# Second table's stage: the routing-weight and gelu tiles are issued from ScalarE's queue instead of SyncE's

## The chip, the cores and the metric

The kernel runs on one core of one Trainium2 chip. The metric is device time in microseconds (us) of one execution of the whole program. Three runs of the kernel before gave a median of 2546.19 us (2545.17 to 2549.54).

## What is computed

One inference step of a one-layer encoder, in float32, for 384 tokens: 256 of a new stream (the prompt) and 8 x 16 of running streams (the sample). The layer is a pooling mixer and a differential attention, then a block of experts that are looked up by key:

```python
q = (xb @ w_pq).reshape(T, PEER_HEADS, 2, D_HALF)
s = jnp.einsum('thcd,ckd->thck', q, sub_keys)
s1, i1 = lax.top_k(s[:, :, 0], PEER_TOPK)
s2, i2 = lax.top_k(s[:, :, 1], PEER_TOPK)
...
g = jax.nn.softmax(best, axis=-1)
u = jnp.take(u_tab, eidx, axis=0)
a = jax.nn.gelu(jnp.einsum('thkd,td->thk', u, xb))
vv = jnp.take(v_tab, eidx, axis=0)
return jnp.einsum('thk,thkd->td', (g * a).astype(xb.dtype), vv)
```

There are 8 heads with 16 experts each, 16384 experts, and rows of 2048 numbers in both tables (`u_tab`, `v_tab`), 134 MB each. Only the last einsum, over the second table `v_tab`, is touched by the change.

## The kernel before, in words

The program runs its engines by hand-written lists: each engine has one function with its own instructions in order and its own waits on semaphores. SyncE (SP), ScalarE (ACT) and GpSimd (POOL) can start DMAs, each on a queue of its own. In the profile SP's is q1, ACT's q10 and POOL's q0.

For the 256 prompt tokens the experts are computed densely. The first table's stage multiplies every row of `u_tab` with every token, applies gelu and writes the result to `a_dense` in HBM. GpSimd meanwhile scatters the routing weights g into `g_dense` in HBM, zero where an expert isn't chosen. The second table's stage then computes y = (g * a) @ v_tab over all 16384 experts, in 128 **blocks** of 128 rows. For the 128 sample tokens the chosen rows of `v_tab` are gathered one expert slot at a time (128 gathers of 128 rows of 8 KB, `v_row`) and added up by VectorE.

One block m of the second table's stage, with `s = m % 4` and, for the pair j = m // 2, `par = j % 2`:

- SP loads 1 MB of `v_tab` into `vraw[s]` (`v_weights`, line 377; the profile calls the four slots `v_raw` and `raw`). A slot is free when VectorE has split block m - 4, so SP waits for `lo_done` (line 408).
- ACT rounds it to `vH[s]` (`v_hi`, line 810: `v_hi` or `ring_hi`), after TensorE has done with block m - 4 (`split_used`).
- VectorE subtracts to get the remainder `vL[s]` (line 1290: `v_lo` or `ring_lo`).
- TensorE does 24 matmuls of 512 columns (`v_step`, lines 1329 to 1331) into all eight banks.

For each pair j of blocks there is one pair of **tiles**: `g_tile` and `a_tile`, 256 KB each, two buffers each (`v_routes`, lines 381 and 382). VectorE multiplies them to `w_tile` (line 1265, behind its split of the even block 2j - 2), ACT rounds the product to `w_hi` (`w_hi`, line 815, behind `v_hi` of block 2j), and VectorE forms `w_lo` (line 1270, behind its split of block 2j - 1). Its fixed order per block is: split of block m; `w_tile` of pair m/2 + 1 if m is even, `w_lo` of that pair if m is odd; one gathered row added (line 1282, from block 4 on).

SP's list in this stage before the change is the part that matters. It first issues blocks 0 to 3 and the tiles of pairs 0 and 1 among the last `a_dense` stores, waits until all those stores have landed (line 401), and then loops:

```python
            sp.wait_ge(a_store[0], 16 * 64)
            sp.wait_ge(a_store[1], 16 * 64)
            with sp.Fori(1, P // VS) as it:
                for par in range(2):
                    sp.wait_ge(w_mult, it * 2 + (par - 1))
                    v_routes(it * 2 + par, par)
                    for q in range(2):
                        s = 2 * par + q
                        sp.wait_ge(lo_done, it * VS + (s + BASE_V - 1))
                        v_weights(it * VS + s, s)
```

So the tiles of pair j stand in q1 ahead of blocks 2j and 2j + 1, and behind blocks 2j - 2 and 2j - 1. GpSimd's gather k waits until row k - 5 has been added (`row_used`, five buffers).

Of the kernel before, what the change touches and what calls it, by code (L numbers as in the profile page):

```python
# [21 lines left out]
P = 128  # L22
# [24 lines left out]
BASE_V = BASE_U  # L47
# [31 lines left out]
TD = SEQ  # L79
# [3 lines left out]
VS = 4  # L83
# [40 lines left out]
def hybrid_layer(nc, I, O):  # L124
    F32, F32R, U32 = mybir.dt.float32, mybir.dt.float32r, mybir.dt.uint32
    ALU, ACT, AX = mybir.AluOpType, mybir.ActivationFunctionType, mybir.AxisListType
    ds = bass.ds
    ctx = ExitStack()
    with ctx:
# [6 lines left out]
        def at(name, kb, shape, dt=F32):  # L136
            return nc.alloc_sbuf_tensor_at(name, shape, dt, offset=base + int(kb * KB))
# [100 lines left out]
        gt = at("g_tile", MX, [P, 2, 2, TD])  # L238
        at_ = at("a_tile", MX + 4, [P, 2, 2, TD])
# [13 lines left out]
        Gd = nc.dram_tensor("g_dense", (P, P, TD), F32, kind="Internal").ap()  # L253
        Ad = nc.dram_tensor("a_dense", (P, P, TU), F32, kind="Internal").ap()
# [3 lines left out]
        def sem(n):  # L258
            names[n] = ctx.enter_context(nc.semaphore(n))
            return names[n]  # L260
# [5 lines left out]
        hi_done, lo_done, split_used = sem("hi_done"), sem("lo_done"), sem("split_used")  # L266
# [21 lines left out]
        a_store = [sem("a_store0"), sem("a_store1")]  # L288
        ag_in = [sem("ag_in0"), sem("ag_in1")]
# [5 lines left out]
        w_mult, wh_done, wl_done, z_done, acc_done, y_done = (sem(x) for x in "w_mult wh_done wl_done z_done acc_done y_done".split())  # L295
# [22 lines left out]
        @block.sync  # L318
        def _(sp):
            def load(n, slot, parts, free):  # L320

                sp.wait_ge(free[0], free[1])
                for dst, src in parts:
                    sp.dma_start(dst, src).then_inc(raw_ready[slot], 16)

            def weight_step(n, slot, w, kq, cols):
                load(n, slot, [(raw[:, slot, k * W:(k + 1) * W], w[(kq * KQ + k) * P:(kq * KQ + k + 1) * P, cols])
                               for k in range(KQ)], (lo_done, n + 1))

            with sp.Fori(0, NG) as g:  # L330
                for s in range(12):
                    if s == 1:
                        sp.wait_ge(x_in[NT - 1], 16)
                    blk, kq = divmod(s, 4)
                    weight_step(g * 12 + s, s % 2, I["w_in"][0], kq, ds(g * GW + DPOOL + blk * DATT, W))
            for kq in range(4):
                weight_step(BASE_POOL + kq, kq % 2, I["w_in"][0], kq, ds(0, W))
            for nb in range(4):
                for i, kq in enumerate(W_OUT_ORDER):
                    weight_step(nb * 4 + (BASE_WOUT + i), i % 2, I["w_out"][0], kq, slice(nb * W, (nb + 1) * W))  # L340

            with sp.Fori(0, 4) as nb:
                for kq in range(4):
                    weight_step(nb * 4 + (BASE_WPQ + kq), kq % 2, I["w_pq"][0], kq, ds(nb * W, W))

            def u_load(m, slot):

                sp.dma_start(rawu[slot], u_v[:, ds(m, 1), :].rearrange("p o d -> p (o d)")).then_inc(u_in[slot], 16)

            def u_next(m, slot):  # L350

                sp.wait_ge(u_turn, m * 2 + (2 - 2 * UR))
                u_load(m, slot)

            def store_gelu(m, k):

                sp.wait_ge(gelu_done, m + 3)
                sp.dma_start(Ad[ds(m, 1), :, :].rearrange("o p x -> (o p) x"), aout[:, k, :]).then_inc(a_store[k], 16)

            sp.wait_ge(split_used, BASE_WPQ + 2)  # L360
            u_load(2, 2)
            u_load(3, 3)
            for m in range(2):
                sp.wait_ge(lo_done, BASE_U + m + 1)
                u_load(m, m)
            for m in range(UR, 2 * UR):
                u_next(m, m % UR)
                if m >= 6:
                    store_gelu(m - 6, m % 2)
            with sp.Fori(2, P // UR) as it:  # L370
                for q in range(UR):
                    u_next(it * UR + q, q)
                    store_gelu(it * UR + (q - 6), q % 2)

            def v_weights(m, slot):

                sp.dma_start(vraw[slot], v_v[:, ds(m, 1), :].rearrange("p o d -> p (o d)")).then_inc(v_in[slot], 16)

            def v_routes(j, par):

                sp.dma_start(gt[:, par, :, :], Gd[ds(j * 2, 2), :, :].rearrange("q p t -> p q t")).then_inc(ag_in[par], 16)
                sp.dma_start(at_[:, par, :, :], Ad[ds(j * 2, 2), :, 0:TD].rearrange("q p t -> p q t")).then_inc(ag_in[par], 16)

            sp.wait_ge(rt_ready, ROUTED)
            v_weights(0, 0)
            v_weights(1, 1)
            for m in range(P - 6, P - 2):
                store_gelu(m, m % 2)
            sp.wait_ge(dot_done, DOTS)
            sp.wait_ge(g_scat, 16 * N_SCATTER)  # L390
            v_routes(0, 0)
            sp.wait_ge(u_turn, 2 * (P - 4) + 2)
            v_weights(2, 2)
            sp.wait_ge(u_turn, 2 * (P - 3) + 2)
            v_weights(3, 3)
            v_routes(1, 1)
            store_gelu(P - 2, 0)
            store_gelu(P - 1, 1)

            sp.wait_ge(a_store[0], 16 * 64)  # L400
            sp.wait_ge(a_store[1], 16 * 64)
            with sp.Fori(1, P // VS) as it:
                for par in range(2):
                    sp.wait_ge(w_mult, it * 2 + (par - 1))
                    v_routes(it * 2 + par, par)
                    for q in range(2):
                        s = 2 * par + q
                        sp.wait_ge(lo_done, it * VS + (s + BASE_V - 1))
                        v_weights(it * VS + s, s)
            sp.wait_ge(row_used, SLOTS)  # L410
            sp.dma_start(y_rows[NT - 1], hh[:, NT - 1, :]).then_inc(y_out, 16)
            for t in range(NT - 1):
                for half in range(2):
                    sp.wait_ge(y_done, 4 * t + 2 * half + 2)
                    cols = slice(half * 2 * W, (half + 1) * 2 * W)
                    sp.dma_start(y_rows[t][:, cols], hh[:, t, cols]).then_inc(y_out, 16)
            sp.wait_ge(y_out, 16 * (1 + 2 * (NT - 1)))
            sp.wait_ge(kv_stored, NG * 96)
            sp.wait_ge(pool_out, 16 * 9)
# [120 lines left out]
        def _(act):  # L540
# [263 lines left out]
            gelu(P - 1, 1)  # L804


            def v_hi(m, s, sets):

                act.wait_ge(v_in[s], sets * 16 + 16)
                A(vH[s], vraw[s], ACT.Copy).then_inc(hi_done, 1)  # L810

            def w_hi(j, par):

                act.wait_ge(w_mult, j + 1)
                A(wth[:, par, :, :], wt[:, par, :, :], ACT.Copy).then_inc(wh_done, 1)

            v_hi(0, 0, 0)
            w_hi(0, 0)
            v_hi(1, 1, 0)
            v_hi(2, 2, 0)  # L820
            w_hi(1, 1)
            v_hi(3, 3, 0)
            with act.Fori(1, P // VS) as it:
                for s in range(VS):
                    act.wait_ge(split_used, it * VS + (s + BASE_V - 1))
                    v_hi(it * VS + s, s, it)
                    if s % 2 == 0:
                        act.wait_ge(split_used, it * VS + (s + BASE_V))
                        w_hi(it * 2 + s // 2, s // 2)


        @block.vector
# [836 lines left out]
```

## Time and profile before

| what | value |
|---|---|
| median of 3 runs | 2546.19 us |
| the profiled execution | 2546.42 us |
| its span in the trace | 2544.8 us |
| second table's stage (first v step to last) | about 1792 to 2536 us |
| busy share of the span | PE 96%, DVE 72%, ACT 37%, POOL 42% |
| granted TensorE clock over the span | 0.993 |
| DMA, whole span | 722.77 MB, mean 284 GB/s |

The profiled execution is 1.6 us longer than its span, and 0.2 us longer than the median. Busy PE is not PE at its peak, since matmuls overlap in the records. Where a line of the profile belongs to a helper function (1329 to 1331, or 1585), it covers several stages, so the stage is read by windows of time.

### The profile page before, as it was taken

To read this page: it belongs to the slowest core of one execution; us is meant where nothing else is said; L and a number is where in the kernel's file an instruction comes from. 1 tells how busy PE (TensorE), PEld (TensorE's weight loads), DVE (VectorE), ACT (ScalarE), POOL (GpSimd) and SP (SyncE) were. 2 spreads that over 40 slices of the span, in tenths; PEclk is the share of its full clock that TensorE was granted. 3 is DMA by queue.
4 is the path that set the end of the run, shared out by engine and by line. 5 is a ranking of instruction groups with operands and counts; after the bars stand their busy time and mean duration, and the time that the engine had idled before them with its cause. 6 is when DMAs were issued, how large, how long until landed. Compare 5 with 4: busy or idle time off the path is not lost.

```text
span 2544.8 us, 41887 instructions
## 1 busy us (share of the span) xinstructions
PE 2444.6 (96%) x15891; PEld 2192.4 (86%) x15891; DVE 1833.0 (72%) x2370; ACT 943.6 (37%) x1158; POOL 1061.8 (42%) x618
## 2 busy tenths in 40 slices
PE   7989999999999999899999999999899999999998
PEld 5878777778999999899999999999787777777777
DVE  3555544554477876788877777776688898888988
ACT  5354543533333333233333333333333334333332
POOL 1020100120006777722577777871344444445441
PEclk9999999999999999999999999999999999999999
DMA  5453544486335666898999999996999999999996
GB/s 192 126 190 117 172 136 142 141 336 238 126 114 144 150 166 179 283 357 333 333 347 344 335 343 338 342 341 249 352 413 411 413 412 412 412 410 412 411 411 280
DMA packets 221525, 722.77 MB, mean 284 GB/s; under 512 B 55672, under 2 KB 105624, under 8 KB 154871
## 3 DMA queue, kind: packets, MB, share of 16 engines
q1 hardware_dynamic: 132304, 397.46, 42.8%
q0 software_dynamic: 87408, 318.89, 35.2%
q10 hardware_dynamic: 1719, 5.26, 0.6%
q8 instruction: 47, 0.77, 0.1%
q14 instruction: 47, 0.39, 0.0%
HBM read 679.70 MB, written 41.83 MB: 284 GB/s over the span
## 4 chain that ended last, share of the span: by engine, by line
PE 60%; DMA 19%; DVE 13%; issue 4%; ACT 1%; SPq 1%; POOL 1%; DVEq 1%; ACTq 0%
PE banks L1329 16%; PE banks L1331 16%; PE banks L1330 16%; DMA a_tile<-a_dense 9%; PE banks L1585 8%; DMA raw<-in_v_tab 5%; DVE h L1282 5%; DVE v_lo L1290 2%; DMA v_raw<-in_v_tab 1%; DMA raw<-in_w_out 1%; DVE ring_lo L1290 1%; DVE ring_lo L860 1%; DVEq L838 1%; DMA a_dense<-gelu_out 1%; POOL g_dense L491 1%
## 5 line engine op out<-in xcount | busy, mean ns | idle before, releaser
L1329 PE MATMUL banks<-xT_hi,ring_hi 128*128 128x256 f32 (+1 forms) x2304 | 686.1, 298 | 11.7 <-DVE gelu_out L1227 10.1
L1331 PE MATMUL banks<-xT_hi,ring_lo 128*128 128x256 f32 (+1 forms) x2304 | 664.0, 288 | 0.0
L1330 PE MATMUL banks<-xT_lo,ring_hi 128*128 128x256 f32 (+1 forms) x2304 | 663.5, 288 | 0.0
L491 POOL DMA_INDIRECT g_dense<-route,route_place x256 | 462.2, 1806 | 306.3 <-DVE route_place L1194 184.6
L528 POOL DMA_INDIRECT v_row<-in_v_tab,route_place x128 | 339.0, 2648 | 428.0 <-DVE h L1282 374.6
L781 ACT ACTIVATE ring_hi<-banks 128x1024 fp32r<-128x1024 f32 x256 | 262.5, 1026 | 625.3 <-PE banks L1585 585.8
L1236 DVE TENSOR_TENSOR ring_lo<-banks,ring_hi 128x1024 fp32r<-128x1024 f32 x256 | 313.1, 1223 | 217.1 <-ACT ring_hi L781 178.4
L1329 PEld LDWEIGHTS banks<-xT_hi,ring_hi 128*128 128x128 f32 x2304 | 439.1, 191 | 13.1 <-DVE ring_lo L1236 12.6
L1330 PEld LDWEIGHTS banks<-xT_lo,ring_hi 128*128 128x128 f32 x2304 | 439.5, 191 | 0.0
L1331 PEld LDWEIGHTS banks<-xT_hi,ring_lo 128*128 128x128 f32 x2304 | 438.8, 190 | 0.0
L860 DVE TENSOR_TENSOR ring_lo<-raw,ring_hi 128x2048 fp32r<-128x2048 f32 x72 | 165.0, 2291 | 219.9 <-ACT ring_hi L556 219.5
L1282 DVE SCALAR_TENSOR_TENSOR h<-v_row,w_values,h 128x2048 f32<-128x2048 f32 x128 | 300.2, 2345 | 0.7
L1243 DVE CUSTOM_DVE_ANT_0 u_row<-u_row,x_rows 128x2048 f32<-128x2048 f32 x128 | 290.3, 2284 | 12.1 <-DMA u_row<-in_u_tab,route_place 10.5
L485 POOL DMA_INDIRECT u_row<-in_u_tab,route_place x128 | 191.5, 1496 | 181.9 <-DVE a_dots L1243 153.2
L1585 PE MATMUL banks<-cst,raw 128*128 128x128 f32 x2032 | 264.0, 273 | 0.0
L1329 PE MATMUL banks<-ring_hi,w_hi 128*128 128x512 f32 x512 | 204.0, 398 | 25.7 <-DVE ring_lo L1290 25.7
L1585 PEld LDWEIGHTS banks<-cst,raw 128*128 128x128 f32 x2032 | 228.5, 140 | 0.0
L1329 PE MATMUL banks<-v_hi,w_hi 128*128 128x512 f32 x512 | 202.3, 395 | 13.6 <-DVE v_lo L1290 13.5
L810 ACT ACTIVATE v_hi<-raw 128x2048 fp32r<-128x2048 f32 x64 | 122.8, 1919 | 229.9 <-DMA raw<-in_v_tab 222.0
L556 ACT ACTIVATE ring_hi<-raw 128x2048 fp32r<-128x2048 f32 x72 | 137.8, 1914 | 180.5 <-PE banks L1331 136.9
L810 ACT ACTIVATE ring_hi<-v_raw 128x2048 fp32r<-128x2048 f32 x64 | 122.8, 1919 | 216.5 <-DMA v_raw<-in_v_tab 214.9
L1330 PE MATMUL banks<-ring_lo,w_hi 128*128 128x512 f32 x512 | 201.6, 394 | 0.0
(248 smaller groups left out, 4012.8 us busy)
## 6 DMA issues: line engine op xcount, KB each, us to landing
raw<-in_u_tab SPq DMA_DIRECT2D x128, 1024.0 KB
v_raw<-in_v_tab SPq DMA_DIRECT2D x64, 1024.0 KB, 15.1
raw<-in_v_tab SPq DMA_DIRECT2D x64, 1024.0 KB
raw<-in_w_in SPq DMA_DIRECT2D x160, 256.0 KB, 3.4
raw<-in_w_out SPq DMA_DIRECT2D x64, 256.0 KB, 4.8
g_dense<-zeros POOLq DMA_DIRECT2D x16, 1024.0 KB, 28.6
raw<-in_w_pq SPq DMA_DIRECT2D x64, 256.0 KB, 3.6
a_dense<-gelu_out SPq DMA_DIRECT2D x128, 128.0 KB
```

Of the source, the lines that this page charges most:

```text
L485: pool.indirect_dma_start(out=urow[i % NUB][:, :], out_offset=None, in_=I["u_tab"][0], in_offset=bass.IndirectOffsetOnAxis(ap=routeU[:, NT ...
L491: pool.indirect_dma_start(out=places, out_offset=bass.IndirectOffsetOnAxis(ap=routeU[:, t, 2, j:j + 1], axis=0), in_=route[:, t, 0, j:j + ...
L528: pool.indirect_dma_start(out=vrow[k % NVB][:, :], out_offset=None, in_=rows, in_offset=bass.IndirectOffsetOnAxis(ap=routeU[:, NT - 1, 1, ...
L781: A(ringH[:, k, g * 2 * W:(g + 1) * 2 * W], psum[:, 2 + 2 * g:4 + 2 * g, :], ACT.Copy).then_inc(u_hi_done, 1)
L810: A(vH[s], vraw[s], ACT.Copy).then_inc(hi_done, 1)
L1236: V.tensor_tensor(ringL[:, k, cols], psum[:, 2 + 2 * g:4 + 2 * g, :].rearrange("p b x -> p (b x)"), ringH[:, k, cols].bitcast(F32), ALU.su ...
L1243: V.tensor_tensor_reduce(row[:, :], row[:, :], xrow[:, :], 1.0, 0.0, ALU.mult, ALU.add, adot[:, i:i + 1]).then_inc(dot_done, 1)
L1282: V.scalar_tensor_tensor(out=acc, in0=vrow[k % NVB][:, :], scalar=wval[:, k:k + 1], in1=acc, op0=ALU.mult, op1=ALU.add).then_inc(row_used, 1)
L1329: MM(out, h1, h2, start=first, stop=False)
L1330: MM(out, h1, l2, start=False, stop=False)
L1331: return MM(out, l1, h2, start=False, stop=last)
L1585: last = TR(bank[2 + b // 4][:, b % 4 * P:(b % 4 + 1) * P], rawu[slot][:, b * P:(b + 1) * P], ident)
```

## The change

The tiles of pairs 2 to 63 are issued by ACT, on ACT's queue. The waits for the `a_dense` stores move with them: ACT has them ahead of pair 2, and SP has them no more. SP's wait on `w_mult` (that the tile's buffer has been multiplied) is dropped, since ACT has waited for the same product in `w_hi`. Pairs 0 and 1 stay with SP.

```diff
@@ SyncE @@
-            sp.wait_ge(a_store[0], 16 * 64)
-            sp.wait_ge(a_store[1], 16 * 64)
             with sp.Fori(1, P // VS) as it:
                 for par in range(2):
-                    sp.wait_ge(w_mult, it * 2 + (par - 1))
-                    v_routes(it * 2 + par, par)
                     for q in range(2):
                         s = 2 * par + q
                         sp.wait_ge(lo_done, it * VS + (s + BASE_V - 1))
@@ ScalarE @@
+            def v_routes(j, par):
+
+                act.dma_start(gt[:, par, :, :], Gd[ds(j * 2, 2), :, :].rearrange("q p t -> p q t")).then_inc(ag_in[par], 16)
+                act.dma_start(at_[:, par, :, :], Ad[ds(j * 2, 2), :, 0:TD].rearrange("q p t -> p q t")).then_inc(ag_in[par], 16)
+
@@ -820,13 +821,24 @@
             w_hi(1, 1)
             v_hi(3, 3, 0)
-            with act.Fori(1, P // VS) as it:
+            for par in range(2):
+                act.wait_ge(a_store[par], 16 * 64)
+            for par in range(2):
+                v_routes(2 + par, par)
+            with act.Fori(1, P // VS - 1) as it:
                 for s in range(VS):
                     act.wait_ge(split_used, it * VS + (s + BASE_V - 1))
                     v_hi(it * VS + s, s, it)
                     if s % 2 == 0:
                         act.wait_ge(split_used, it * VS + (s + BASE_V))
                         w_hi(it * 2 + s // 2, s // 2)
+                        v_routes(it * 2 + (s // 2 + 2), s // 2)
```

The last round of the loop is written out behind it, without `v_routes`.

SyncE's list at the end of the first table's stage and the start of the loop over the second table, before (L358 is the store of gelus, L377 a block, L381 and L382 the tiles):

```order
L377 DMA raw<-in_v_tab 128x2048 [waits u_turn] x2
L381 DMA g_tile<-g_dense 128x2x256
L382 DMA a_tile<-a_dense 128x2x256
L358 DMA a_dense<-gelu_out 128x256 [waits gelu_done] x2
L402 UNCONDITIONAL_BRANCH [waits a_store1,a_store0]
L402 ISA
L381 ISA [waits w_mult]
L381 DMA g_tile<-g_dense 128x2x256
L382 DMA a_tile<-a_dense 128x2x256
L408 ISA
L377 ISA [waits lo_done]
L377 DMA v_raw_122<-in_v_tab 128x2048
```

And with the change:

```order
L377 DMA raw<-in_v_tab 128x2048 [waits u_turn] x2
L381 DMA g_tile<-g_dense 128x2x256
L382 DMA a_tile<-a_dense 128x2x256
L358 DMA a_dense<-gelu_out 128x256 [waits gelu_done] x2
L400 UNCONDITIONAL_BRANCH
L400 ISA
L377 ISA [waits lo_done]
L377 DMA v_raw_122<-in_v_tab 128x2048
```

Block 4 (the last row) now waits for `lo_done` alone, and neither the two waits nor a tile stand ahead of it.

ScalarE's list from block 3 into its loop, with the change (L811 is `v_hi`, L816 `w_hi`, L805 and L806 the tiles):

```order
L811 ACTIVATE v_hi_125<-raw 128x2048 [waits v_in3]
L805 DMA g_tile<-g_dense 128x2x256 [waits a_store1,a_store0]
L806 DMA a_tile<-a_dense 128x2x256
L805 DMA g_tile<-g_dense 128x2x256
L806 DMA a_tile<-a_dense 128x2x256
L828 UNCONDITIONAL_BRANCH
L828 ISA
L810 ISA [waits split_used]
L811 ACTIVATE ring_hi<-v_raw_122 128x2048 [waits v_in0]
```

The tiles of pairs 2 and 3 now go out together, ahead of the rounding of block 4. Later in the same list, one half of a round:

```order
L816 ACTIVATE w_hi<-w_tile 128x512 [waits w_mult]
L805 ISA
L805 DMA g_tile<-g_dense 128x2x256
L806 DMA a_tile<-a_dense 128x2x256
L811 ACTIVATE ring_hi<-v_raw_123 128x2048 [waits v_in1,split_used]
```

Two DMA issues now stand between the rounding of the product and the rounding of the odd block.

## Rows read from the trace of the kernel before

**Rows 1.** The page's chain of waits that ended last, by line.

```profile
PE banks L1329 16%; PE banks L1331 16%; PE banks L1330 16%; DMA a_tile<-a_dense 9%; PE banks L1585 8%; DMA raw<-in_v_tab 5%; DVE h L1282 5%; DVE v_lo L1290 2%; DMA v_raw<-in_v_tab 1%; DMA raw<-in_w_out 1%; DVE ring_lo L1290 1%; DVE ring_lo L860 1%; DVEq L838 1%; DMA a_dense<-gelu_out 1%; POOL g_dense L491 1%
```

**Rows 2.** Windows: us, busy us of each engine, granted clock, DMA share, GB/s.

```profile
1840.00:2500.00 660.00, 630.75 (x2716) 509.72 (x2715) 587.98 (x345) 246.48 (x170) 318.50 (x118) 0.99 1.02 412
2500.00:2505.00 5.00, 5.00 (x23) 4.13 (x22) 4.39 (x2) 1.92 (x1) 2.55 (x1) 1.00 1.02 423
```

**Rows 3.** Waits, 1700 to 2545 us: engine, for whom: us, times, longest.

```profile
ACT v_hi L810 <- DMA raw<-in_v_tab: 222.0, 58, 8.9
ACT ring_hi L810 <- DMA v_raw<-in_v_tab: 214.9, 61, 8.7
DVE w_tile L1265 <- DMA a_tile<-a_dense: 55.2, 29, 7.3
DVE w_lo L1270 <- ACT w_hi L815: 33.3, 32, 4.4
```

**Rows 4.** Groups by line, 1820 to 2520 us: busy, mean ns, idle before.

```profile
L1329 PE MATMUL banks<-ring_hi,w_hi 128*128 128x512 f32 x483 | 191.5, 396 | 17.5 <-DVE ring_lo L1290 17.5
L1329 PE MATMUL banks<-v_hi,w_hi 128*128 128x512 f32 x480 | 189.8, 395 | 12.2 <-DVE v_lo L1290 12.1
```

**Rows 5.** DMA queues, 1900 to 2500 us: packets, MB, share of 16 engines.

```profile
q1 hardware_dynamic: 42999, 134.74, 57.1%
q0 software_dynamic: 15390, 112.06, 45.2%
```

**Rows 6.** Window 1800 to 1830 us, and the first five of it.

```profile
1800.00:1830.00 30.00, 28.03 (x124) 22.90 (x123) 24.21 (x17) 13.07 (x9) 5.49 (x2) 1.00 0.89 312
1800.00:1805.00 5.00, 3.03 (x14) 2.19 (x13) 5.00 (x4) 2.43 (x2) 0.00 (x0) 1.00 0.37 141
```

**Rows 7.** Timeline of SP's queue at the stage's start: start us, us, what.

```profile
1782.20 5.14 SPq L358 DMA_DIRECT2D a_dense<-gelu_out  x2
1803.04 0.41 SPq L381 DMA_DIRECT2D g_tile<-g_dense  x1
...
1804.24 0.96 SPq L377 DMA_DIRECT2D v_raw<-in_v_tab  x2
...
1816.89 5.80 SPq L377 DMA_DIRECT2D v_raw<-in_v_tab  x2
```

**Rows 8.** Timeline of VectorE at the stage's start; in brackets idle before, releaser.

```profile
1789.92 2.28 DVE L1290 TENSOR_TENSOR ring_lo<-v_raw,ring_hi 128x2048 fp32r<-128x2048 f32 x1
...
1806.51 0.69 DVE L1265 TENSOR_TENSOR w_tile<-a_tile,g_tile 128x512 f32<-128x512 f32 x1 [1.28 <-DMA a_tile<-a_dense]
1807.12 2.28 DVE L1290 TENSOR_TENSOR v_lo<-raw,v_hi 128x2048 fp32r<-128x2048 f32 x1
1813.83 0.69 DVE L1270 TENSOR_TENSOR w_lo<-w_tile,w_hi 128x512 fp32r<-128x512 f32 x1 [4.43 <-ACT w_hi L815]
1814.44 2.28 DVE L1290 TENSOR_TENSOR ring_lo<-v_raw,ring_hi 128x2048 fp32r<-128x2048 f32 x1
```

**Rows 9.** Timeline of ScalarE, block 4 and the product of pair 2.

```profile
1811.36 1.92 ACT L810 ACTIVATE ring_hi<-v_raw 128x2048 fp32r<-128x2048 f32 x1 [8.67 <-DMA v_raw<-in_v_tab]
1813.18 0.61 ACT L815 ACTIVATE w_hi<-w_tile 128x512 fp32r<-128x512 f32 x1
```

**Rows 10.** Timeline of TensorE, first matmul of block 1.

```profile
1802.48 0.50 PE L1329 MATMUL banks<-ring_hi,w_hi 128*128 128x512 f32 x1 [1.97 <-DVE ring_lo L1290]
```

**Rows 11.** Timeline of SP's queue and of ScalarE in steady running.

```profile
2006.99 0.42 SPq L382 DMA_DIRECT2D a_tile<-a_dense  x1
...
2006.11 0.62 ACT L815 ACTIVATE w_hi<-w_tile 128x512 fp32r<-128x512 f32 x1
2008.38 1.92 ACT L810 ACTIVATE v_hi<-raw 128x2048 fp32r<-128x2048 f32 x1 [1.65 <-DMA raw<-in_v_tab]
```

**Rows 12.** DMA in 1300 to 1400 us, first table's stage: queue and issues.

```profile
q1 hardware_dynamic: 3836, 16.09, 42.5%
...
raw<-in_u_tab SPq DMA_DIRECT2D x13, 1024.0 KB
a_dense<-gelu_out SPq DMA_DIRECT2D x14, 128.0 KB
```

More of the change, by code:

```diff
@@ L829, in _ @@
                         w_hi(it * 2 + s // 2, s // 2)
+                        v_routes(it * 2 + (s // 2 + 2), s // 2)
+            for s in range(VS):
+                act.wait_ge(split_used, P - VS + s + BASE_V - 1)
+                v_hi(P - VS + s, s, P // VS - 1)
+                if s % 2 == 0:
+                    act.wait_ge(split_used, P - VS + s + BASE_V)
+                    w_hi(P // 2 - 2 + s // 2, s // 2)
         @block.vector
```

## The prediction

> **What bounds the kernel now.** I read the chain of waits first. It names the change's own transfer: the loads of `a_tile` hold 9% of the span [rows 1], 229 us, which looks like a prize. Before believing it I ask what those loads wait for, so the windows of the second table's stage come next. From 1840 to 2500 us the 16 DMA engines are busy 1.02 of the time and move 412 GB/s, while PE shows 0.96 (630.75 of 660) and DVE 0.89 [rows 2]. A full DMA share that doesn't move for 660 us is a bound. The bytes agree: a block moves 1.049 MB of the table, 1.049 MB of gathered rows and half of 0.524 MB of tiles, 2.36 MB, which at 412 GB/s is 5.73 us, and 128 of these make 733 us of the some 744 that the stage takes. The waits say the same from the other side: ACT stands 222.0 + 214.9 us for blocks, against DVE's 55.2 us for tiles and 33.3 us for `w_hi` [rows 3]. PE's idle time in this stretch is only 17.5 + 12.2 = 29.7 us [rows 4].
>
> So the tile is late because it stands in q1 behind two blocks, two megabytes, in a stage whose DMA engines are full. If it passes them, somebody else's bytes wait.
>
> **Steady running: the rate.** The change removes no byte and no packet. SP issues the 62 pairs of tiles no more, two issues of some 0.42 us each [rows 11]; SP is on no path there. The time of the issue hardly moves either. SP begins `a_tile` at 2006.99, right behind `g_tile`; ACT would begin the two behind `w_hi`, which ends at 2006.73 [rows 11]. What moves is the queue. On q10 the tile shares the engines with q1 and q0 instead of standing behind q1's blocks, and lands sooner. DVE's 55.2 us of waits for tiles then go, and what is late next is the block: ACT waits longer for it, `w_hi` stands behind that block's rounding in ACT's list, and DVE waits at `w_lo` in place of `w_tile`. I cost steady running at **0 us**. The cover is the full DMA share; were it gone, the gain would end where PE is never idle, 29.7 us.
>
> ACT gains two issues for each of 62 pairs, about 0.9 us with the gap between them, in front of the rounding of the odd block. That rounding waited 1.65 us for its data in the sample that I read [rows 11], so this lies in idle time: **0 us**. Without that cover it would be 62 x 0.9 = 56 us, which is why it is worth watching.
>
> **The start of the stage.** Here the change takes a wait away. From 1800 to 1830 us the DMA engines move 312 GB/s, and only 141 in the first five [rows 6]. Against 412 that is 30 x (1 - 312/412) = **7.3 us of DMA time lost**. The cause is in SP's list: the last store is issued by 1787, then SP stands for the stores to land until 1803.04, and block 4 goes out at 1804.24 [rows 7]. Its slot was free when DVE had split block 0, at 1789.92 + 2.28 = 1792.2 [rows 8]. With the change it goes out there, 12 us sooner. The engines are still full then, so it queues and fills the hole as it opens.
>
> - Block 4 in the hole: 1.05 MB at 412 GB/s, **2.5 us** of DMA time.
> - The next loads: before, block 4 was rounded only at 1811.36 after 8.67 us of waiting, and `w_hi` behind it at 1813.18 [rows 9]. That held DVE 4.43 us at `w_lo` and put the split of block 4 at 1814.44 to 1816.7 [rows 8]. Block 8 is released by it, at 1816.89 [rows 7], and so is the first added row and through it gather 5. With the change block 4 lies ready. `w_hi` then waits for PE to end block 1: 1802.48 [rows 10] plus 5.4 us (24 matmuls at 28.03/124 = 0.226 us each [rows 6]), so 1807.9, and it ends at 1808.5. DVE ends its split of block 3 at 1807.12 + 2.28 = 1809.4, does `w_lo` (0.69) and the split of block 4 (2.28), and is through at 1812.3 [rows 8]. Block 8 is 4.6 us sooner. But the tiles of pair 2, alone in q1 before (1803.04 to 1806.5), now share with blocks 4 and 5, which can cost them up to a block's 2.5 us, and DVE's product at 1806.51 waits for them. So the lead is 2.1 to 4.6 us, and I take the middle, **3.4 us**.
> - The tiles pass blocks: each block lands later by what a pair of tiles takes, 0.524 MB / 412 = 1.3 us. That is one shift, not one for each pair, since the total is the same; it costs once, at the end: **-1.3 us**.
>
> PE's own start doesn't move: block 1 waits for DVE's split of it, which stands behind the product of pair 1, and those tiles stay in q1. From 1802.48 PE runs without a gap to 1830 (28.03 of the 30 us, [rows 6]). It needs 5.4 us for a block against the DMA's 5.73, so it has room to take the lead over.
>
> Sum: 2.5 + 3.4 - 1.3 = 4.6 us. At the ends: if only the small lead counts, 2.1 - 1.3 = 0.8 us; if the whole hole is filled at no cost, 7.3 us. The profiled execution took 2546.42 us, so I forecast 2546.4 - 4.6 = **2541.8 us**; the median of the runs is 0.2 us under the profiled one, which I leave out.
>
> **The rivals.**
>
> *Nothing comes of it.* The tiles change queues, the engines are the same, and what block 4 gains is eaten at once: the tiles of pairs 2 and 3, now issued together, pass blocks 4 and 5 and delay them by 2 x 1.3 us, and the shift at the end takes another 1.3. For it: both pairs come at the worst time, with DVE waiting for one of them. Against it: the hole of 7.3 us is real, and its loads are ready. From my 4.6 us another 2.6 and up to the whole 3.4 of the lead go, so 2545 to 2547, say 2546. Chance 0.10. The Trainium skill (DMA: Bandwidth & Descriptors, section Issuing engines are not separate DMA queues) states this as a rule: DMAs started by ScalarE, SyncE and GpSimd run on the same 16 DMA engines and interleave, and spreading them saves only the time of issuing. By that rule alone the sum would be 0; the full share of the steady stretch agrees with it, while the hole at the start is a matter of when SP gets to issue, which the rule allows for.
>
> *The DMA share is not a true ceiling.* DVE's late tile would then be what holds back the next loads, and 412 GB/s what the requests ask for. For it: 423 GB/s from 2500 to 2505 [rows 2], and tiles are what DVE waits for at the end of many chains. Against it: the share is full in every window. At 423 the 660 us would take 660 x 412/423 = 643, 17 us less, so 2546.4 - 4.6 - 17 = 2525; the far end is PE's 29.7 us, 2512. Chance 0.10.
>
> *A third queue makes small packets dearer: slower.* Tiles travel in pieces of 1 KB, 512 to a pair. On q0, 112.06 MB are 13,680 pieces of 8 KB, and 0.452 x 16 x 600 us make 317 ns for each. On q1 four fifths of the bytes are blocks, 13,160 such pieces; its 0.571 x 9600 us less those leave 1,310 us for some 26,300 pieces of 1 KB, 50 ns each [rows 5]. Among the scatters of the first table's stage, the same sum for 13 blocks and 14 stores leaves (680 - 527) us for 1,792 pieces, 85 ns [rows 12]. So company can change the price. Each ns more costs 512/16 = 32 ns a pair, 2 us over 62 pairs. The gain is gone at 2.3 ns more, and the change is slower by 0.2% at 5 ns. At a quarter of the way to 85 (9 ns) it costs 18 us: 2541.8 + 18 = 2560; at the far end 70 us. Against it: those were writes beside scatters of single numbers, and these are the same reads beside the same gathers as now. Chance 0.14, nearly all of it slower.
>
> **How the numbers follow.** A measurement of this kernel can tell about 0.2% from no change, 5.1 us. My own case has 0.66. Its gain runs from 0.8 to 7.3 us, around 4.6, and passes 5.1 in a little under half: 0.30 faster, 0.36 the same. The first rival adds 0.10 to the same, the second 0.10 to faster, the third 0.13 to slower and 0.01 to the same. That makes 0.40 faster, 0.47 the same, 0.13 slower. The forecast stays with its own sum, which lies just inside the same. For 8 in 10 the range takes my case (2539.1 to 2545.6), the first rival (to 2547), and a little of the other two on each side, 2535 to 2549.
>
> **What the changed profile would show.** Block 4 issued near 1792 instead of 1804.24; the window 1800 to 1830 near 400 GB/s instead of 312; `w_lo` of pair 2 and the split of block 4 some 2 to 4.6 us sooner; q10 with 33 MB more; DVE's waits for `a_tile` near nothing, those of `w_lo` longer by about as much, and ACT's for blocks unchanged at some 437 us; 412 GB/s as before in steady running; the last block's load and the end some 4 to 5 us sooner. I am wrong if the steady rate leaves 410 to 414 GB/s: upward the second rival, downward the third. I am wrong about ACT if PE comes to wait on the odd blocks more than on the even ones.

## The result and the profile after

The change makes the kernel slower: 2607.77 us (median of 4 runs, 2604.78 to 2608.68) against 2545.68 us, a ratio of 1.0243 with a 95% interval of 1.023 to 1.0255. That is 62 us, and far outside the range of 2535 to 2549. The profiled execution took 2608.68 us, its span 2607.1 us.

The two windows of [rows 2] and [rows 6] and the DMA queues of [rows 5], now. First the windows (us, busy us of each engine, granted clock, DMA share, GB/s):

```profile
1800.00:1805.00 5.00, 5.00 (x23) 4.12 (x24) 2.58 (x2) 0.88 (x2) 0.00 (x0) 1.00 1.01 402
1800.00:1830.00 30.00, 27.41 (x114) 22.26 (x115) 21.85 (x16) 10.78 (x8) 5.50 (x3) 0.94 0.90 314
1840.00:2500.00 660.00, 595.78 (x2488) 484.26 (x2487) 534.65 (x315) 229.82 (x156) 291.11 (x108) 0.95 0.96 377
```

The steady stretch, which I had costed at nothing, moves 377 GB/s instead of 412, and the DMA engines are busy 0.96 of the time instead of 1.02. The stage's 302 MB take 801 us at 377 and 733 at 412: 68 us more, somewhat over the 62 measured. From 1800 to 1830 us the rate is that of before (314 against 312), so the time was lost in steady running, by DMA engines that stand idle.

Queues, 1900 to 2500 us (packets, MB, share of 16 engines):

```profile
q0 software_dynamic: 14256, 103.82, 42.0%
q1 hardware_dynamic: 13537, 98.58, 41.7%
q10 hardware_dynamic: 25475, 24.56, 12.1%
```

q10 carried 24.56 MB in 12.1% of 16 x 600 us. That is 48 ns for each 1 KB piece, where [rows 5] gave 50 ns in q1. The DMA records of the trace, taken one by one from 1900 to 2500 us, have a mean of 48 ns in both. A small piece is not dearer on a third queue. Now the waits of [rows 3] (the lines have moved by 12 in VectorE's list):

```profile
ACT w_hi L816 <- PE banks L1343: 156.2, 37, 8.2
DVE w_tile L1277 <- DMA a_tile<-a_dense: 152.7, 24, 10.4
ACT w_hi L816 <- DVE w_tile L1277: 126.3, 24, 10.0
ACT ring_hi L811 <- DMA v_raw<-in_v_tab: 101.7, 33, 6.4
ACT v_hi L811 <- DMA raw<-in_v_tab: 97.2, 33, 6.3
```

VectorE waits 152.7 us for the tiles that were to come early, 55.2 before. ACT waits 199 us for blocks, 437 before. The blocks are early now and the tiles late.

One such wait in order of time. The chain of waits, then the timelines of ACT and VectorE (start us, us, what, in brackets idle before and releaser):

```profile
1994.96 25.28 DMA a_tile<-a_dense
...
1994.96 0.94 ACTq L806 DMA_DIRECT2D a_tile<-a_dense  x1
...
2009.96 2.29 DVE L1302 TENSOR_TENSOR ring_lo<-v_raw,ring_hi 128x2048 fp32r<-128x2048 f32 x1
2020.26 0.69 DVE L1277 TENSOR_TENSOR w_tile<-a_tile,g_tile 128x512 f32<-128x512 f32 x1 [8.01 <-DMA a_tile<-a_dense]
```

The tile takes 25 us to land. In the kernel before, such loads stand in the chain with 15 to 19 us, two of them here:

```profile
1996.06 16.20 DMA a_tile<-a_dense
...
2018.96 17.19 DMA a_tile<-a_dense
```

With the change VectorE stands for 8 of the 25 us, and since it releases the blocks and the gathers, both other queues run empty behind it. Two windows show the end of that:

```profile
2010.00:2020.00 10.00, 10.00 (x46) 8.28 (x45) 2.25 (x2) 1.92 (x1) 2.75 (x1) 1.00 1.03 418
2020.00:2030.00 10.00, 6.03 (x18) 4.48 (x17) 9.74 (x6) 4.34 (x3) 4.19 (x2) 0.74 0.66 251
```

After the stall the DMA share is 0.66, TensorE works 6 of 10 us, and its granted clock in that window is 0.74. The clock is a second part of the price, and it lies on the way to the next tile. After the stall before this one:

```profile
1986.97 0.63 PE L1341 MATMUL banks<-v_hi,w_hi 128*128 128x512 f32 x1 [3.12 <-DVE v_lo L1302]
...
1987.00:1990.00 3.00, 3.00 (x8) 2.32 (x9) 3.00 (x3) 1.87 (x1) 0.73 (x1) 0.53 0.92 313
1991.00:1994.00 3.00, 3.00 (x15) 2.48 (x14) 3.00 (x3) 0.00 (x0) 1.79 (x1) 1.00 1.00 399
```

TensorE had stood 3.12 us for VectorE's split. Its granted clock is 0.53 at first (the lower level, 1.2 of 2.4 GHz, for nearly all of it) and 1.00 from 1991 on. The first matmuls start 0.43 us apart, later ones 0.23. The block's 24 matmuls take 7.2 us (1986.97 to 1994.13) instead of the 5.4 that 24 x 0.23 make. ACT rounds the product behind them at 1994.34, and only then issues the tile of 1994.96. The chain of waits from 1840 to 2500 us has 16 such loads of `a_tile`, of 24 to 31 us. At 1.8 us each the lower clock would account for up to 29 of the 62 us. That is an estimate, and no run separates it from the wait that sets it off.

Why 25 us for half a megabyte? The queues in 2012 to 2021 us, when all three had work, and in 2022 to 2032 us, when the other two had little:

```profile
q0 software_dynamic: 235, 1.79, 47.8%
q1 hardware_dynamic: 231, 1.75, 46.9%
q10 hardware_dynamic: 217, 0.21, 6.7%
...
q1 hardware_dynamic: 148, 1.07, 26.0%
q0 software_dynamic: 118, 0.93, 22.3%
q10 hardware_dynamic: 646, 0.62, 19.6%
```

In the first window the three queues moved about the same number of pieces, 235, 231 and 217 (with a few records of 4 bytes in each), but the two others' were of 8 KB and q10's of 1 KB. That gave the first theory.

### The profile page after: what moved, and what is told of

It reads as the page before. It is cut to its first block, busy times and chain, and to the rows that moved or that the text cites. A ratio compares the mean times of both kernels' runs of the same rounds, so it can differ in the third digit from the quotient of the medians.

```text
span 2607.1 us, 41846 instructions
## 1 busy us (share of the span) xinstructions
PE 2465.8 (95%) x15891; PEld 2213.7 (85%) x15891; DVE 1829.0 (70%) x2370; ACT 948.8 (36%) x1158; POOL 1062.2 (41%) x618
## 3 DMA queue, kind: packets, MB, share of 16 engines
q0 software_dynamic: 87408, 318.89, 34.4%
## 4 chain that ended last, share of the span: by engine, by line
PE 69%; DMA 19%; DVE 8%; issue 2%; POOL 1%; DVEq 1%; ACT 0%; ACTq 0%; SPq 0%
PE banks L1341 19%; PE banks L1343 19%; PE banks L1342 19%; DMA a_tile<-a_dense 18%; PE banks L1597 8%; DVE h L1294 2%; DVE v_lo L1302 1%; DVE ring_lo L1302 1%; DVEq L850 1%; DMA a_dense<-gelu_out 1%; POOL g_dense L487 1%; DMA raw<-in_w_in 0%; DVE prm L952 0%; DVE prm L979 0%; PE banks L1548 0%
## 5 line engine op out<-in xcount | busy, mean ns | idle before, releaser
L1341 PE MATMUL banks<-xT_hi,ring_hi 128*128 128x256 f32 (+1 forms) x2304 | 686.0, 298 | 13.0 <-DVE gelu_out L1239 11.5
L1341 PEld LDWEIGHTS banks<-xT_hi,ring_hi 128*128 128x128 f32 x2304 | 439.0, 191 | 14.4 <-DVE ring_lo L1248 14.0
L1341 PE MATMUL banks<-v_hi,w_hi 128*128 128x512 f32 x512 | 208.4, 407 | 45.1 <-DVE v_lo L1302 45.1
L1342 PE MATMUL banks<-v_lo,w_hi 128*128 128x512 f32 x512 | 206.7, 404 | 0.0
L1343 PE MATMUL banks<-v_hi,w_lo 128*128 128x512 f32 x512 | 205.8, 402 | 0.0
L1343 PE MATMUL banks<-ring_hi,w_lo 128*128 128x512 f32 x512 | 205.3, 401 | 0.0
```

Source lines behind the costliest of these rows:

```text
L1341: MM(out, h1, h2, start=first, stop=False)
L1342: MM(out, h1, l2, start=False, stop=False)
L1343: return MM(out, l1, h2, start=False, stop=last)
```

## The theories

**A.** Each DMA engine takes one piece from each queue in turn. A pair of tiles is 512 pieces, 32 for each engine, so beside two full queues it needs 32 x (317 + 317 + 50) ns = 21.9 us and a latency. The stage wants a pair every 11.5 us. In SyncE's queue the tile's pieces stood one behind the other, and a pair of tiles competed with one other queue, not two.

Equal counts alone would also fit turns of several pieces each. The start times of the records settle it. Of the pieces that end between 2012 and 2021 us on q0, 86% have a q1 piece start within 5 ns of their end. Behind q1's it is a q10 piece (84%), and behind q10's a q0 piece (93%). A piece of the same queue follows in 9 to 12% of cases, which is chance. So the order is q0, q1, q10, q0, one piece each.

The tile lands with the slowest of the 16 DMA engines. From 1998 to 2002 us q10 had 485 records beside q0's 88 and q1's 66, and some 460 of the 512 pieces of the pair issued at 1994.5 had started by then. Yet the pair hadn't landed. In 2002 to 2009 us:

```profile
q0 software_dynamic: 203, 1.52, 52.0%
q1 hardware_dynamic: 185, 1.38, 47.3%
q10 hardware_dynamic: 30, 0.03, 1.2%
```

At one piece in 0.684 us these 30 are the work of about three DMA engines. (The trace doesn't name the engine of a record, so this is inferred.) The pair's first piece starts at 1998.0, and 32 turns from there end at 2019.9. VectorE starts at 2020.26. So the 21.9 us are the time of a DMA engine whose other two queues never run short. From 1840 to 2500 us the median `a_tile` landed after 18.8 us, and 21 of 52 took more than 20.

**B.** The moment of the issue costs. It now stands behind ACT's wait for TensorE (156.2 us in all). The start times in the traces speak against it. From the end of a product to the issue of the tiles that reuse its buffer it was 5.5 us in the mean before, and it is 1.5 us with the change. From there to the product that needs these tiles it was 17.3 us, and it is 23.4. So the tiles are issued earlier, and come later.

**C.** Small pieces are dearer on a third queue. That was the slower rival of the prediction; the 48 ns above speak against it.

## Experiments

All ratios are against runs of the kernel before on the same chip. Their median was 2547.49 us for the first four kernels of the table, 2545.22 us for act_512 and real_act_start, and 2547.35 us for the others. The ratio is not the quotient of the two medians, and can differ from it by 0.1%; small gains below are worked out from the ratio. All but act_512 and act_early lie within 2% of the kernel before with the whole interval.

| kernel | runs | median us | ratio, 95% interval |
|---|---|---|---|
| sp_after_whi | 8 | 2546.61 | 0.9993 (0.9981 to 1.0004) |
| act_wide | 5 | 2532.55 | 0.9933 (0.9917 to 0.9948) |
| act_half_blocks | 5 | 2557.04 | 1.0035 (1.002 to 1.0051) |
| act_early | 2 | 2587.77 | 1.0157 (1.0099 to 1.0216) |
| act_512 | 2 | 2678.29 | 1.0522 (1.0503 to 1.0542) |
| block4_first | 12 | 2542.25 | 0.9986 (0.9975 to 0.9997) |
| real_act | 6 | 2533.34 | 0.9945 (0.993 to 0.9961) |
| real_sp | 8 | 2535.52 | 0.996 (0.9947 to 0.9974) |
| real_sp_block4 | 6 | 2535.56 | 0.9958 (0.9942 to 0.9974) |
| real_act_start | 6 | 2529.67 | 0.9933 (0.992 to 0.9946) |

### The moment alone: sp_after_whi

```diff
-                    sp.wait_ge(w_mult, it * 2 + (par - 1))
+                    sp.wait_ge(wh_done, it * 2 + (par - 1))
```

> The kernel before, with one semaphore changed: SyncE issues the tiles of pair j + 2 only once ScalarE has rounded the product of pair j (as late as ScalarE does it with the change), but still in SyncE's own queue, in line with the blocks. Theory A (the queue is what costs: on a queue of its own a tile moves one 1 KB piece each time that the two other queues move 8 KB each, so it lands some 24 us after its issue instead of 16): the tiles stay in line, so this stays within 5 us of the kernel before, 2541 to 2551 us. Theory B (the moment is what costs: the issue now stands behind ScalarE's waits for TensorE, 156 us in all): this loses most of what the change loses, 2590 to 2610 us.

Measured: no difference. Its steady stretch is the old one:

```profile
1840.00:2500.00 660.00, 631.08 (x2709) 509.82 (x2708) 587.75 (x343) 245.77 (x169) 317.19 (x118) 0.99 1.02 412
```

In SyncE's queue the issue can wait for ACT's rounding and nothing is lost. As a test of B it is weak, though, since the new wait seldom held anything up. SyncE's waits, 1840 to 2500 us:

```profile
SPq L381 <- ACT w_hi L815: 11.0, 14, 1.6
```

The mean from a product to the issue went from 5.5 to 5.7 us only. What tells against B by itself is that the changed kernel has 1.5 us there.

### Half as many pieces: act_wide

```diff
-                act.dma_start(gt[:, par, :, :], Gd[ds(j * 2, 2), :, :].rearrange("q p t -> p q t")).then_inc(ag_in[par], 16)
+                act.dma_start(gt[:, par, :, :].rearrange("p q t -> p (q t)"), Gd[ds(j * 2, 2), :, :].rearrange("q (h r) t -> (q h) (r t)", r=2)).then_inc(ag_in[par], 16)
```

and the same for `a_tile`. The numbers land in other places, so this kernel shows the time only.

> The changed kernel, with the 62 pairs of tiles on ScalarE's queue read as 2 KB for each partition instead of twice 1 KB: the same bytes in half as many pieces (the numbers land in other places, so the result isn't the reference's). Theory A: half as many turns, 16 for each DMA engine instead of 32, each of 317 + 317 + about 90 ns, so 12 us and the fixed latency; the tile is no longer late, VectorE's waits for a_tile fall from 152.7 us to under 40, and the time comes back to 2540 to 2555 us. Theory B: pieces change nothing, 2600 to 2610 us. A third theory, C (a 1 KB piece costs a DMA engine more when it comes from a third queue): the DMA share stays, half of the extra goes, 2570 to 2580 us.

Measured: 75 us came back, 13 more than the change had lost. Waits for tiles, then q10 from 1900 to 2500 us:

```profile
DVE w_tile L1277 <- DMA a_tile<-a_dense: 34.4, 22, 10.2
...
q10 hardware_dynamic: 15110, 27.51, 12.1%
```

Same bytes, same queue, same issue, half the turns. A gives the direction and the 34.4 us; it does not give a time below the kernel before. That part is taken up by real_sp.

### The other queue's pieces halved: act_half_blocks

```diff
-                sp.dma_start(vraw[slot], v_v[:, ds(m, 1), :].rearrange("p o d -> p (o d)")).then_inc(v_in[slot], 16)
+                src = v_v[:, ds(m, 1), :].rearrange("p o d -> p (o d)")
+                for c in range(2):
+                    sp.dma_start(vraw[slot][:, c * 2 * W:(c + 1) * 2 * W], src[:, c * 2 * W:(c + 1) * 2 * W]).then_inc(v_in[slot], 16)
```

ACT's wait for a block counts both halves.

> The changed kernel, with each block of the second table loaded by two DMAs of half its columns: 4 KB pieces on SyncE's queue instead of 8 KB, the tiles untouched. Theory A: a turn of the three queues now takes about 317 + 160 + 50 = 527 ns instead of 684, so the tile lands after 32 x 0.527 = 17 us instead of 22 to 25; its waits fall by more than half and the time to 2550 to 2585 us (the blocks get fewer bytes a turn, so not all of it comes back). Theories B and C: no gain, 2600 us or more.

Measured: 51 us came back with the tiles untouched. This is the test I trust most, since nothing about the tiles, their queue or their issue differs from the changed kernel. The steady window and q1 from 1900 to 2500 us:

```profile
1840.00:2500.00 660.00, 626.48 (x2693) 503.94 (x2692) 580.20 (x339) 242.47 (x167) 314.88 (x117) 0.99 1.03 407
...
q1 hardware_dynamic: 29243, 106.48, 45.0%
```

The DMA share is full again, and VectorE waits for `a_tile` 3 times and 14.4 us in all. What is left, 407 against 412 GB/s, is the price of the 4 KB pieces: 4,320 us for 26,000 of them, 166 ns each, against half of 317. 302 MB at 407 take 9 us longer, and the kernel is 9.5 us slower than its kernel before.

### The issue ahead of the wait for TensorE: act_early

```diff
+                        act.wait_ge(w_mult, it * 2 + (s // 2 + 1))
+                        v_routes(it * 2 + (s // 2 + 2), s // 2)
                         act.wait_ge(split_used, it * VS + (s + BASE_V))
                         w_hi(it * 2 + s // 2, s // 2)
-                        v_routes(it * 2 + (s // 2 + 2), s // 2)
```

> The changed kernel, with ScalarE issuing the tiles of pair j + 2 as soon as pair j has been multiplied, ahead of its wait for TensorE and of the rounding. Theory A: the queue still moves one pair in 22 to 25 us whenever the other two are full, so a head start of a few us helps a part only: 2575 to 2605 us. Theory B: the late issues are gone, 2541 to 2560 us.

Measured: 20 of the 62 us came back by the median. There are two runs, 2582.11 and 2593.44 us, and the interval allows 7 to 37 us. In the faster one, VectorE still waits 124.6 us for tiles, and the DMA share is 0.98:

```profile
DVE w_tile L1278 <- DMA a_tile<-a_dense: 124.6, 21, 10.8
...
1840.00:2500.00 660.00, 608.85 (x2578) 495.79 (x2577) 556.00 (x327) 235.18 (x161) 302.42 (x113) 0.96 0.98 389
```

So the moment counts once the queue is slow, for about a third, known only roughly. The chain shows how: in the changed kernel product, issue and landing follow each other on it, and an earlier issue shortens that round.

### Twice as many pieces: act_512

Each of the tile DMAs is cut in two by columns, on both engines:

```diff
+                for c in range(2):
+                    cs = slice(c * P, (c + 1) * P)
+                    act.dma_start(gt[:, par, :, cs], Gd[ds(j * 2, 2), :, cs].rearrange("q p t -> p q t")).then_inc(ag_in[par], 16)
```

> The changed kernel with every tile DMA cut in two by columns, so that ScalarE's queue carries 512 B pieces, twice as many, of the same bytes. Theory A: a pair needs 64 turns instead of 32, each of 317 + 317 us/1000 and some 30 to 40 ns, 42 us while both other queues are full, against the 11.5 us in which the stage wants a pair; the DMA engines stand idle far more often, DMA share under 0.9, and the loss against the kernel before grows from 60 us to well over 150: 2700 to 2950 us. If instead the price of a small piece were only its own time on the engine, 512 more pieces of 30 ns are under 1 us a pair, 2610 to 2670 us.

Measured: 2678 us, 133 us over the kernel before instead of 62. The loss about doubled, but I had expected well over 150, so A's range, from 2700 us on, missed by 22 us at its near end. The other range, to 2670, missed by 8, so the time alone doesn't decide. VectorE's waits for `a_tile` rose from 152.7 to 221.8 us, and from 1840 to 2500 us the DMA share is 0.90, at 344 GB/s. My sum of turns leaves out that VectorE's stall empties the other queues and the tile then runs freely. That this is the whole reason for the miss is not shown. The turns themselves show well. Queues in 2010 to 2020 us, and two issues on ACT's queue:

```profile
q0 software_dynamic: 281, 2.04, 49.2%
q1 hardware_dynamic: 276, 2.00, 48.2%
q10 hardware_dynamic: 261, 0.13, 4.6%
...
2009.36 10.22 ACTq L809 DMA_DIRECT2D g_tile<-g_dense  x1
2019.67 2.08 ACTq L810 DMA_DIRECT2D a_tile<-a_dense  x1
```

The counts are equal again, 281, 276 and 261, with q10's pieces now of 512 B: 0.13 MB against 2.0. Half the size, half the bandwidth. The order of the starts is the same as well, q0, q1, q10, in about eight of ten.

### The start alone: block4_first

On the kernel before; the first round of the loop is written out behind this, without its block 4:

```diff
+            sp.wait_ge(lo_done, VS + BASE_V - 1)
+            v_weights(VS, 0)
             sp.wait_ge(a_store[0], 16 * 64)
             sp.wait_ge(a_store[1], 16 * 64)
```

> The kernel before, with one thing that the change did by the way and nothing else: SyncE issues block 4 as soon as block 0 has been split, ahead of its wait for the a_dense stores. The tiles stay in SyncE's queue. The prediction's own term: block 4 fills 2.5 us of the hole in the DMA traffic and the blocks behind it lead by up to 4.6 us, so 2.5 to 6 us faster than the kernel before, ratio 0.9976 to 0.999. The rival: what block 4 gains is eaten by the later blocks, ratio 0.999 to 1.001. The hole itself should show 380 GB/s or more from 1800 to 1830 us instead of 312 either way if block 4 was what it lacked.

```profile
1800.00:1830.00 30.00, 29.82 (x131) 24.68 (x132) 25.80 (x19) 13.30 (x10) 8.24 (x3) 1.00 0.99 356
...
1808.29 2.29 DVE L1300 TENSOR_TENSOR ring_lo<-v_raw,ring_hi 128x2048 fp32r<-128x2048 f32 x1
```

Measured: 0.14% faster (0.03 to 0.25%), 3.5 us, and 356 GB/s in the hole where I had written 380 or more. The split of block 4 starts at 1808.29 in this execution, 6 us before that of [rows 8], but the whole start of the stage lay some 2 us earlier here, so the lead is 4 us.

### A layout with 2 KB pieces: real_act, real_sp, real_sp_block4, real_act_start

`g_dense` and `a_dense` are laid out by partition, block, token, so that a pair's tile is one run of 2 KB for each partition. The scatter's place becomes i1 * 128 + i2, and no instruction is added:

```diff
-                V.scalar_tensor_tensor(out=place, in0=i2, scalar=float(P), in1=i1, op0=ALU.mult, op1=ALU.add)
+                V.scalar_tensor_tensor(out=place, in0=i1, scalar=float(P), in1=i2, op0=ALU.mult, op1=ALU.add)
...
-                sp.dma_start(Ad[ds(m, 1), :, :].rearrange("o p x -> (o p) x"), aout[:, k, :]).then_inc(a_store[k], 16)
+                sp.dma_start(Ad[:, ds(m, 1), :].rearrange("p o x -> p (o x)"), aout[:, k, :]).then_inc(a_store[k], 16)
...
-                act.dma_start(gt[:, par, :, :], Gd[ds(j * 2, 2), :, :].rearrange("q p t -> p q t")).then_inc(ag_in[par], 16)
+                act.dma_start(gt[:, par, :, :].rearrange("p q t -> p (q t)"), Gd[:, ds(j * 2, 2), :].rearrange("p q t -> p (q t)")).then_inc(ag_in[par], 16)
```

real_act is the changed kernel so, real_sp the kernel before so, real_sp_block4 is real_sp with block4_first's start. real_act_start is real_act with that start, and pairs 2 and 3 stay with SyncE.

> The changed kernel with g_dense and a_dense laid out by partition, then block, then token, so that a tile reads 2 KB in one piece for each partition, and all numbers are the reference's. Theory A (a queue gets turns by pieces): as with the permuted 2 KB reads, VectorE's waits for a_tile under 40 us and 2528 to 2540 us, unless the first table's stage suffers from scatters and stores that now lie further apart; that is seen in the window 1100 to 1700 us, which has 341 GB/s and a full TensorE before.

> The same layout on the kernel before: the tiles in 2 KB pieces, in SyncE's queue. From the shares of the queues a 1 KB piece costs a DMA engine about 50 ns and a 2 KB piece should cost 80 to 90, so a pair saves (512 x 50 - 256 x 85)/16 = 0.24 us less than nothing to 0.35 us, over 62 pairs 10 to 20 us: 2526 to 2537 us. If that is what the faster run with 2 KB pieces on ScalarE's queue had, the two kernels with this layout agree within 4 us, and ScalarE's queue brings nothing of its own. If its early landing is worth something by itself, this one is 5 us or more slower than the other.

> The 2 KB layout in SyncE's queue together with block 4 ahead of the store waits. If the two gains add, it is 2.5 to 6 us below real_sp and the fastest of all; if block 4 brings nothing it equals real_sp.

> The 2 KB layout with the tiles on ScalarE's queue from pair 4 on; block 4 goes out early as in block4_first, and pairs 2 and 3 stay in SyncE's queue, where pair 2 isn't held up by the blocks and gathers of two other queues (VectorE waited 11.72 us for it with the tiles of pair 2 on ScalarE's queue). If the two parts add, 5 to 8 us less than real_act, 2524 to 2530 us and the fastest of all; if the start doesn't matter, as real_act, about 2533 us. From 1800 to 1830 us it should move about 360 GB/s as block4_first does.

The steady window of real_sp and its q1, then that of real_act:

```profile
1840.00:2500.00 660.00, 634.86 (x2752) 514.80 (x2751) 595.12 (x348) 248.35 (x171) 322.39 (x120) 1.00 1.02 417
...
q1 hardware_dynamic: 29947, 136.29, 55.9%
```

```profile
1840.00:2500.00 660.00, 642.66 (x2781) 527.19 (x2781) 603.11 (x352) 254.17 (x174) 317.99 (x120) 0.98 1.02 417
```

Both have 417 GB/s at a full DMA share. By the sum of [rows 5], real_sp's pieces of 2 KB cost 86 ns where two of 1 KB cost 100; by the single records it is 86 against 96. The 302 MB take 724 us at 417 against 733, 9 us, and real_sp is 0.4% faster than its kernel before, 10 us. That explains most of what act_wide had below the kernel before. Whether ACT's queue brings something of its own on top stays open: real_act is at 0.9945 and real_sp at 0.996, and their intervals overlap; the medians are 2.2 us apart, inside the 4 us that I had set for "nothing of its own". The first table's stage, 1100 to 1700 us, keeps its 341 GB/s in real_act and has 338 in real_sp's profiled execution.

real_sp_block4 is not faster than real_sp by these runs, so the start's gain did not add there. real_act_start is the fastest by its median, 0.67% below the kernel before (0.54 to 0.8%), 17 us (16 by the medians); against real_act (0.9945) the intervals overlap too, so of the 5 to 8 us that I expected of the start 3 are seen and none is sure. The wait that it removes is plain, though. VectorE for pair 2 in real_act:

```profile
1811.46 0.69 DVE L1277 TENSOR_TENSOR w_tile<-a_tile,g_tile 128x512 f32<-128x512 f32 x1 [11.72 <-DMA a_tile<-a_dense]
```

and the start's window went from 311 GB/s (real_act) to 348 in real_act_start:

```profile
1800.00:1830.00 30.00, 28.60 (x126) 23.35 (x125) 23.06 (x17) 13.19 (x9) 5.50 (x2) 1.00 0.94 348
```

## Why the prediction was wrong

**The step that failed** is the one headed "Steady running: the rate", with its "I cost steady running at 0 us", and in it the sentence that a tile on q10 "shares the engines with q1 and q0 instead of standing behind q1's blocks, and lands sooner". The prediction has no figure for "sooner"; behind it stood a share of the bytes, a third for each queue, by which 0.52 MB take some 4 us. What the engines share out is turns, one piece each. A queue of 1 KB pieces gets an eighth of what a queue of 8 KB pieces gets, 0.21 MB against 1.75 in 9 us. The tiles that stand in the chain land after 24 to 31 us, where they took 15 to 19. The steady rate fell from 412 to 377 GB/s, and the step that I had put at 0 us cost the 62. The Trainium skill (DMA: Bandwidth & Descriptors, section Queues, rings and completion order) says that a DMA engine goes round between its queues a packet at a time, typically 9 to 17 descriptors. By that a pair's 32 pieces would go in two to four turns, an estimate from the page's figure at one descriptor a piece. The order of the starts from 2012 to 2021 us disagrees, with one DMA record of each queue in turn in 84 to 93% of cases, and the measurement decides.

**The full DMA share as cover** was read rightly and used wrongly. It says that no byte can go faster; it does not say that the engines stay full. I had asked what holds the rate up and not what would let it fall. The loads that VectorE waits for decide when the others are released, so their lateness empties the queues. I had named "what is late next", and had it on the wrong resource: not the block, the tile itself.

**The start.** Block 4 was issued at 1791.21 to fill the hole, as forecast, and the first five us went from 141 to 402 GB/s. Over 30 us the rate stayed at 314 (312 before, [rows 6]), because the tile of pair 2 held VectorE: it came at 1810.65, not at 1806.5. I had allowed 2.5 us for that and it cost 4.1. The split of block 4 starts at 1814.06, 0.4 us sooner than in [rows 8], where I had 2.1 to 4.6. Alone, block4_first gave 3.5 us, against 2.5 + 3.4 = 5.9 us of my sum without the shift: right in kind, high by 2.4 us.

**ACT's two issues** were costed at 0 in idle time, and that held; the gap in front of the roundings behind them ("issue" as releaser) is 23.9 us in all, beside 199 us in which ACT waits for blocks. My sign of being wrong about ACT did come up: by the trace TensorE stands 74.0 us in front of odd blocks and not at all in front of even ones (22.6 and 10.3 before; gaps over 0.1 us). But it points at the tile. VectorE has its product, which waits for the tile, in front of its split of the odd block.

**The slower rival** forecast slower by a dearer piece, and at its far end 70 us, close to the 62 measured. It was right about the sign by accident: the piece costs 48 ns on q10, 50 before. The sign "downward the third" fitted a fall of the rate whose cause was another. The rival *nothing comes of it* is out by the 62 us. *The share is not a ceiling* wanted 423 GB/s once the tiles are in time; act_half_blocks had nearly all in time and moved 407. Only other piece sizes moved the full-share rate (417 with 2 KB tiles, 407 with 4 KB blocks).

**The chances** gave slower 0.13. A queue that a transfer is moved to deserves its own line of arithmetic, and with it this case would have stood at the head: 32 pieces a DMA engine, two other queues of 8 KB pieces, 317 ns each, all in [rows 5].

## What to carry to other kernels

Before moving a transfer to another queue, count its pieces for each DMA engine and multiply by the turn of all queues that are full then; if that is longer than the time in which it is needed, it falls behind for as long as the other queues stay full. Transfers with small pieces are safest in line in a queue with others, or with larger pieces: here 2 KB instead of 1 KB, by a layout that costs no instruction, turned a loss of 2.4% into a gain of 0.55%. And a full resource hides a change only as long as what feeds it isn't made later.

## What the runs showed of the hardware

- Three full DMA queues are served piece by piece in turn, in the order q0, q1, q10 and at all three sizes seen on q10: 235, 231 and 217 records in 9 us with 8, 8 and 1 KB, and 281, 276 and 261 in 10 us with 8, 8 and 0.5 KB. With 8, 8 and 2 KB (act_wide, 2100 to 2130 us) the order of the starts is the same in 81 to 90% of cases.
- A transfer lands with the slowest of its 16 DMA engines, as inferred from the counts: some 460 of a pair's 512 pieces had started 7.5 us after its issue, and it landed after 25 us.
- A DMA issue can hold its engine: in act_512 one of ACT's issues took 10.22 us (0.38 to 0.43 usually), and ACT's roundings had 150.1 + 123.1 us of "issue" before them. I had no such term. What it adds to that kernel's loss is not separated.
- A piece costs a DMA engine 317 ns with 8 KB, 166 with 4 KB, 86 with 2 KB, 48 to 50 with 1 KB and, from act_512's q10 (13.2% of 9,600 us for 22.79 MB), 28 ns with 512 B.
- In the stretches after a stall the granted TensorE clock is lower: 0.53 from 1987 to 1990 us, behind 3.12 us without work, and 1.00 from 1991 to 1994; 0.74 from 2020 to 2030 us. Over its 660 us the changed kernel has 0.95, against 0.99 before.
